# Re-ordering branch C of a two-layer decoder step: sample products into a gate, one linear between all pairs of levels

## The reference, cut to what matters

```
mix = gates_0 * (h_a @ w_pa) + gates_1 * (h_b @ w_pb) + gates_2 * (h_c @ w_pc)
x   = x + mix @ w_o
x   = x + (silu(gt) * up) @ w_down
```

## Time and profile before

| what | value |
| --- | --- |
| runs, us | 2079.83, 2083.93, 2085.56 (median 2083.93) |
| profiled execution, us | 2087.43 |
| its span, first to last instruction, us | 2085.4 |
| mean granted TensorE clock | 0.989 |
| instructions | 49973 |
| HBM traffic | 307.08 MB read, 12.08 MB written |

### The profile page before, as it was taken

The page is one execution under the profiler, slowest core; times in us unless marked ns, Lnnn a source line. Parts: engine busy times, 40 slices in busy tenths (PEclk is TensorE's granted clock), DMA queues, the critical chain, the costliest instruction groups (busy, mean ns, idle before and its releaser), DMA issues.

```text
span 2085.4 us, 49973 instructions
## 1 busy us (share of the span) xinstructions
PE 2038.4 (98%) x21064; PEld 1929.0 (92%) x21064; DVE 1043.7 (50%) x1611; ACT 720.2 (35%) x1135; POOL 298.0 (14%) x534
## 2 busy tenths in 40 slices
PE   8899999999999999999999999999999999999998
PEld 8888888889999999999998888888899999999998
DVE  7766523365756444433366654233666564444324
ACT  4444214156433222222234431142653332222221
POOL 0202456510000000000001034646000000000000
PEclk9999999999999999999999999999999999999999
DMA  6415999962333333333343279999414333333332
GB/s 220 125 56 167 305 345 335 344 205 72 128 102 91 93 91 92 92 89 89 98 161 103 83 232 301 354 315 356 128 56 136 103 91 89 99 91 92 86 93 77
DMA packets 165558, 322.44 MB, mean 155 GB/s; under 512 B 24420, under 2 KB 104855, under 8 KB 164823
## 3 DMA queue, kind: packets, MB, share of 16 engines
q10 hardware_dynamic: 46944, 147.87, 23.2%
q1 hardware_dynamic: 93814, 100.04, 14.6%
q0 software_dynamic: 24576, 71.34, 9.8%
HBM read 307.08 MB, written 12.08 MB: 153 GB/s over the span
## 4 chain that ended last, share of the span: by engine, by line
PE 85%; DVE 8%; ACT 3%; DMA 2%; issue 1%; ACTq 0%; SPq 0%; DVEq 0%
PE PS L1791 25%; PE PS L1793 24%; PE PS L1792 24%; PE PS L2034 3%; PE PS L2064 3%; DVE wl L686 1%; PE PS L2039 1%; PE PS L1844 1%; DMA vpg<-in_cache_vals 1%; ACT P L1461 1%; PE PS L1830 1%; DVE P L859 1%; DVE PTl L693 1%; DVE kxl L693 1%; DMA raw<-in_wpack 1%
## 5 line engine op out<-in xcount | busy, mean ns | idle before, releaser
L1791 PE MATMUL PS<-hh,wh 128*128 128x260 f32 x3008 | 865.4, 288 | 7.5 <-DVE wl L686 7.2
L1793 PE MATMUL PS<-hl,wh 128*128 128x260 f32 x3008 | 853.0, 284 | 0.0
L1792 PE MATMUL PS<-hh,wl 128*128 128x260 f32 x3008 | 852.2, 283 | 0.0
L1791 PEld LDWEIGHTS PS<-hh,wh 128*128 128x128 f32 x3008 | 570.1, 190 | 22.4 <-issue 13.2
L1793 PEld LDWEIGHTS PS<-hl,wh 128*128 128x128 f32 x3008 | 570.1, 190 | 0.0
L1792 PEld LDWEIGHTS PS<-hh,wl 128*128 128x128 f32 x3008 | 570.0, 189 | 0.1
L686 DVE TENSOR_TENSOR wl<-raw,wh 128x1024 fp32r<-128x1024 f32 (+4 forms) x326 | 359.4, 1103 | 315.3 <-ACT wh L1356 314.5
L1356 ACT ACTIVATE wh<-raw 128x1024 fp32r<-128x1024 f32 (+4 forms) x326 | 304.8, 938 | 464.2 <-PE PS L1793 454.0
L1791 PE MATMUL PS<-fh,wh 128*128 128x260 f32 x704 | 199.3, 283 | 0.0
L1793 PE MATMUL PS<-fl,wh 128*128 128x260 f32 x704 | 198.7, 282 | 0.0
L1792 PE MATMUL PS<-fh,wl 128*128 128x260 f32 x704 | 198.6, 282 | 0.0
(11 more groups left out here) (352 smaller groups left out, 3025.4 us busy)
## 6 DMA issues: line engine op xcount, KB each, us to landing
raw<-in_wpack ACTq DMA_DIRECT2D x238, 512.0 KB, 3.6
vpg<-in_cache_vals SPq DMA_DIRECT2D x256, 128.0 KB, 6.3
vpg<-in_cache_vals POOLq DMA_DIRECT2D x256, 128.0 KB, 5.4
kpg<-in_cache_keys SPq DMA_DIRECT2D x224, 144.0 KB, 4.3
kpg<-in_cache_keys POOLq DMA_DIRECT2D x112, 144.0 KB, 4.8
ky<-in_cache_keys POOLq DMA_DIRECT2D x96, 144.0 KB, 4.2
raw<-in_wpack ACTq DMA_DIRECT2D x48, 256.0 KB, 3.1
raw<-in_wpack ACTq DMA_DIRECT2D x16, 384.0 KB, 3.1
```

Of the source, the lines that this page charges most:

```text
L1791: pe.matmul(out, w[0], x[0], start=first, stop=False)
L1792: pe.matmul(out, w[1], x[0], start=False, stop=False)
L1793: return pe.matmul(out, w[0], x[1], start=False, stop=last)
```

## The change

It re-orders. No product, copy or transfer is added or taken away. In TensorE's queue oh and Ks0 move into g01, behind its fifth block of rows; then each pair of levels is followed by one linear: P00, g02, P01, g03, P02, g04, P03 (before: g01 L0 to L3 P00 and so on, with the sample products between levels). Kt is followed by g05, U by P04, oc0 by g06, the first sums by oc1 and P05, the second sums by g07. The list of groups is changed alike, so the banks move. VectorE's and ScalarE's queues are written anew to match; ScalarE's `sample_read(0)` comes ahead of the decays of its step, and its `head_guesses(0)` behind `outputs(1)` and `head_squares(1)`.

```diff
--- before.py
+++ after.py
@@ -291,21 +291,22 @@
 
     groups.extend(["Vt0", "Vt1", "D0", "D1", "Ot"])
     lin("g01")
-    between = (["oh", "Ks0"], ["P00", "Us0"], ["Ks1", "g02", "os0"], ["P01", "Us1"], ["g03", "os1"], ["P02"], ["g04"])
+    groups.extend(["oh", "Ks0"])
+    between = (["P00", "Us0"], ["Ks1", "g02", "os0"], ["P01", "Us1"], ["g03", "os1"], ["P02"], ["g04"], ["P03"])
     for n, names in enumerate(between):
         groups.extend([f"L{2 * n}", f"L{2 * n + 1}"])
         for name in names:
             (lin if name[0] in "gP" else groups.append)(name)
     groups.extend(["Kt0", "Kt1"])
-    lin("P03")
+    lin("g05")
     groups.extend(["U0", "U1"])
-    lin("g05")
+    lin("P04")
     groups.append("oc0")
-    lin("P04")
+    lin("g06")
     groups.extend(["no00", "no01", "oc1"])
-    lin("g06")
+    lin("P05")
     groups.extend(["no10", "no11"])
-    lin("P05", "g07", "P06", "P07", "g20", "g21")
+    lin("g07", "P06", "P07", "g20", "g21")
     for m in range(8):
         lin(f"P2{m}")
         if m < 6:
@@ -1141,39 +1142,30 @@
                 for k in range(2):
                     rows = brl[0][:, 2 * k:2 * k + 2, 0:TP]
                     lo(f"ha{k}", [(rows, rows.bitcast(F32), brh[0][:, 2 * k:2 * k + 2, 0:TP])])
+                sample_output()
+                spread_queries()
                 gate(0, 1)
                 for n in range(7):
                     if n < 5:
                         near(2 * n)
                         near(2 * n + 1)
-                    if n == 0:
-                        sample_output()
-                        spread_queries()
-                        weights(si["P00"])
-                    if n == 1:
-                        gated(0)
-                        sample_state(0)
+                    if n in (1, 3):
+                        merged(0, n // 2)
+                        sample_state(n // 2)
+                    elif n == 5:
+                        merged(0, 2)
+                    weights(si[("P00", "g02", "P01", "g03", "P02", "g04", "P03")[n]])
                     for i in (2 * n + 4, 2 * n + 5):
                         decayed(i)
                         if i + 3 < 16:
                             difference(i + 3)
-                    if n == 2:
-                        weights(si["g02"])
-                        gate(0, 2)
-                    elif n == 3:
-                        gated(1)
-                        sample_state(1)
-                    elif n == 4:
-                        weights(si["g03"])
-                        gate(0, 3)
-                    elif n == 5:
-                        gated(2)
-                    elif n == 6:
-                        weights(si["g04"])
-                        gate(0, 4)
+                    if n in (1, 3, 5):
+                        gate(0, 2 + n // 2)
+                merged(0, 3)
                 for p in range(2):
                     evac(f"Kt{p}", kbts[p][:, :, :].rearrange("p a b -> p (a b)"), bank(f"Kt{p}"))
-                gated(3)
+                weights(si["g05"])
+                gate(0, 5)
                 for p in range(2):
                     Sall = Salls[p]
                     dve.memset(Sall[:, 0, :], 0.0).then_inc(*mark("dve_step"))
@@ -1217,22 +1209,20 @@
                 def head_low(p, e, y):
                     lo(f"hc{p}{e}", [(brl[2][:, 2 * p + e, :], y[:, :], brh[2][:, 2 * p + e, :])])
 
-                weights(si["g05"])
-                gate(0, 5)
                 gated(4)
+                weights(si["g06"])
+                gate(0, 6)
                 head_variances(0)
+                weights(si["P05"])
                 head_roots(0)
                 ys = [head_output(0, e) for e in range(2)]
-                weights(si["g06"])
+                merged(0, 5)
                 for e in range(2):
                     head_low(0, e, ys[e])
-                gate(0, 6)
                 head_variances(1)
-                weights(si["P05"])
+                weights(si["g07"])
                 head_roots(1)
                 ys = [head_output(1, e) for e in range(2)]
-                merged(0, 5)
-                weights(si["g07"])
                 for e in range(2):
                     head_low(1, e, ys[e])
                 weights(si["P06"])
@@ -1657,50 +1647,53 @@
                 for p in range(2):
                     act.wait_ge(*upto(f"pe Vt{p}"))
                     act.activation(Vts[p][:, :, :, :].rearrange("p (a c) v w -> p a (c v w)", a=2), pair(f"Vt{p}", 512), ACT.Copy).then_inc(*mark("act_evac", f"free Vt{p}"))
+                weights(si["g01"])
+                for k in range(2):
+                    rows = brl[0][:, 2 * k:2 * k + 2, 0:TP].bitcast(F32)
+                    hi(f"ha{k}", [(brh[0][:, 2 * k:2 * k + 2, 0:TP], rows)], ["ha back"])
+                hi("ysm", [(brh[0][:, :, TP:T], ysm[:, :, :])], ["free oh"])
+                sample_keys(0)
+                gate(0, 1)
                 for n in range(7):
-                    weights(si[("g01", "P00", "g02", "P01", "g03", "P02", "g04")[n]])
+                    weights(si[("P00", "g02", "P01", "g03", "P02", "g04", "P03")[n]])
                     if n == 0:
-                        for k in range(2):
-                            rows = brl[0][:, 2 * k:2 * k + 2, 0:TP].bitcast(F32)
-                            hi(f"ha{k}", [(brh[0][:, 2 * k:2 * k + 2, 0:TP], rows)], ["ha back"])
-                        gate(0, 1)
-                        weights(si["P00"])
-                        hi("ysm", [(brh[0][:, :, TP:T], ysm[:, :, :])], ["free oh"])
-                        sample_keys(0)
                         decayed_state(0)
+                    elif n == 2:
+                        sample_read(0)
                     for i in (2 * n + 7, 2 * n + 8):
                         if i < 18:
                             decays(i)
-                    if n == 2:
+                    if n == 1:
                         sample_keys(1)
+                        gate(0, 2)
+                    elif n == 2:
                         decayed_state(1)
-                        gate(0, 2)
-                        sample_read(0)
+                    elif n == 3:
+                        gate(0, 3)
                     elif n == 4:
-                        gate(0, 3)
                         sample_read(1)
                     elif n == 5:
                         far(10)
                         far(11)
+                        gate(0, 4)
                     elif n == 6:
                         far(12)
                         far(13)
-                        gate(0, 4)
                 for p in range(2):
                     collected(p)
-                weights(si["P03"])
+                weights(si["g05"])
                 gate(0, 5)
+                weights(si["P04"])
                 outputs(0)
                 head_squares(0)
-                weights(si["P04"])
-                head_guesses(0)
+                weights(si["g06"])
+                gate(0, 6)
                 outputs(1)
                 head_squares(1)
-                weights(si["g06"])
+                head_guesses(0)
+                weights(si["P05"])
                 head_high(0)
-                weights(si["P05"])
                 head_guesses(1)
-                gate(0, 6)
                 weights(si["g07"])
                 head_high(1)
                 weights(si["P06"])
@@ -2256,35 +2249,38 @@
                 for k in range(2):
                     ins = turn(bank("Ot")[:, 128 * k:128 * k + 128], Oacc[:, 128 * k:128 * k + 128])
                 ins.then_inc(*mark("group_ready", "pe Ot"))
-                gate(0, 1)
+                def sample_part():
+                    sample_output()
+                    sample_keys(0)
+
+                gate(0, 1, {4: sample_part})
                 for n in range(7):
                     level(2 * n)
                     level(2 * n + 1)
                     if n == 0:
-                        sample_output()
-                        sample_keys(0)
-                    elif n == 1:
                         branch(0, 0)
                         sample_update(0)
-                    elif n == 2:
+                    elif n == 1:
                         sample_keys(1)
                         gate(0, 2, {4: lambda: sample_read(0)})
-                    elif n == 3:
+                    elif n == 2:
                         branch(0, 1)
                         sample_update(1)
+                    elif n == 3:
+                        gate(0, 3, {4: lambda: sample_read(1)})
                     elif n == 4:
-                        gate(0, 3, {4: lambda: sample_read(1)})
+                        branch(0, 2)
                     elif n == 5:
-                        branch(0, 2)
+                        gate(0, 4)
                     else:
-                        gate(0, 4)
+                        branch(0, 3)
                 for p in range(2):
                     begin(f"Kt{p}")
```

(9 more changed lines are left out.)

## The result

The changed kernel takes **2118.57 us** (median of 4 runs, 2116.19 to 2121.34), the kernel before beside it 2084.24 (4 runs, 2079.83 to 2085.56). The ratio is 1.0165, with an interval of 1.0146 to 1.0184: slower by 34 us, where 2117 were forecast. The profiled execution's span is 2119.7 us, 34.3 more than before, at a mean granted clock of 0.983 where it had been 0.989.

A forecast was written before the change was run, and what follows sets the result against it. TensorE, busy for 98% of the span, was taken to bound the kernel. Waits of +35.7 us, less 3.2 and 1.6, with clock -7 + 9.2, made +33, so a median of 2117 us; range 2102 to 2128.

The forecast's parts named there:

- the clock: TensorE's half-rate falls behind three pauses per layer: 4.6 us per layer, 9.2 in all, against 7 us of old ones removed.
- b): First level pairs: Ks1 waits for merged(0, 0), g02 for the addition of sample_state(0); 2.8 us lost per layer.
- c): After L6, L7: g03 takes P01's banks and waits for merged(0, 1) behind VectorE's copies; 1.4 us per layer.
- d): L10 takes os1's banks and waits for sample_read(1), put behind decays(15) and decays(16) on ScalarE; 1.6 us per layer.
- f): Heads, counted from T0, oc0's end: VectorE waits for ScalarE, making P06, P07 and g20 late; 11.9 us per layer.
- e): First sample read ahead of decays on ScalarE: Us1's copy comes in time, so 3.2 us of waits go.
- g): Costed at nothing: Kt, g05, U, P04, oc0, weight loads, the second half of S0 and POOL's clearing of blocks.
- The table load: On ScalarE: 1.28 us followed by its activation with no drain; with the skill's drain f would be 1.4 longer per layer.
- VectorE's work alone as what sets the heads: Rival 1: VectorE's own work makes g20 4.5 us late per layer, the sum 14.8 less; 2102 us, chance 0.08.
- The rival of 6.8 us falls: Rival 4: the falls of the clock are 6.8 us long behind each pause; 2128 us, chance 0.10.
- The faster rival: Rival 2: VectorE frees Ks1's and g02's banks and splits g20 in time, leaving 12 us of gains; 2072 us, chance 0.06.
- That gains and losses cancel: Rival 3: f vanishes, and a to d cost 12 us against 12 of gains; 2084 us, chance 0.04.

The follow-up runs named there:

- run with merge first: The changed kernel with merged and sample_state of the levels put ahead of the two near copies in VectorE's queue: 2104.21 us, ratio 1.0095.
- the run that takes this step alone: The kernel before with only sample_read(0) moved ahead of the state's scaling and the gate: 2080.55 us, ratio 0.9994.
- the exchange on ScalarE: The changed kernel with head_guesses(0) and the split of P06 ahead of outputs(1) and head_squares(1) in ScalarE's queue: 2105.21 us, ratio 1.0106.
- the run with the heads' queues mended: The changed kernel, TensorE's order kept, with splits of P06, P07, g20, g21, first guesses and P05's merge ahead of head work not needed yet: 2094.43 us.
- the one with only the heads: The kernel before with its old levels, but P03 ahead of Kt and the changed kernel's heads: 2110.51 us, ratio 1.013.
- the run with the old heads: The changed kernel's levels with the order of the kernel before from Kt on, in all queues: 2094.04 us, ratio 1.0053.
- the last run: The changed kernel's levels with merges and sample reads put forward, and the old order from Kt on: 2076.76 us, ratio 0.9968.
- The three runs with mended levels: The changed kernel with level merges and sample reads put forward; heads mended (2075.63 us), also P20 and g22 splits earlier (2073.41), or old heads (2076.76).

## Why the prediction was right, point by point

The direction and the places were right, and the total too; that the total is so close is in part luck, as the clock below shows. By its terms, per layer, forecast against measured in the first layer:

| term | forecast, us | measured, us |
| --- | --- | --- |
| a) L1 behind g01's gate read | 0.15 | 0.10 |
| b) Ks1, then g02 | 2.8 | 1.37 + 1.07 = 2.44 |
| c) g03 | 1.4 | 1.37 |
| d) L10 | 1.6 | 1.16 |
| f) P06, P07, g20 | 3.1, 2.3, 6.5 | 2.89, 2.02, 4.72 |
| sum of waits | 17.85 | 14.70 |
| clock, both layers, net | +2 | about +9 |

**b)** The order of VectorE's queue is as read: two copies, product, addition. The run with merge first shows it, for it removes the waits by an exchange in that queue alone. g02 starts 3.24 us behind L3's end (461.80 to 465.04), forecast 3.25. The two waits together are 0.4 smaller only because Ks1, at half rate, takes 0.80 us of it instead of 0.42.

**c)** holds to 0.03.

**d)** The releaser is right. The chain from g03's end to the copy took 5.51 instead of 5.8, beside 4.35 of TensorE instead of 4.2. Only the size was off, by 0.44.

**e)** In the changed kernel it is right: undoing it costs 11.7 us. But the sum books the -3.2 as a gain of its own, and the run that takes this step alone gains nothing that shows. A wait that is removed brings TensorE sooner to the next group, where 1.35 us of the 3.2 came back.

**f)** P06, P07 and g20 start 23.88, 29.01 and 38.36 us behind T0; the forecast had 23.8, 29.0 and 38.4. The chain through ScalarE's squares, table load and guesses into VectorE's queue is shown by the exchange on ScalarE, which cuts the idle time from 7.28 to 1.95 and leaves g20's wait. The three waits are 2.3 us less than forecast although the starts came as forecast, for two reasons: P07 ran at half rate and hides 1.5 of g20's, and TensorE's own work up to g20 is 27.2 instead of 26.5 (33.64 from T0 to P07's end, less 2.89, 2.02 and 1.5).

**g)** holds: the stretch has no wait that is not in the table.

**The table load.** The earlier trace rows do not show what the forecast reads from them: the activation behind that load, which they leave out, starts at 522.35, 1.64 us after the load's end, and waits for VectorE. The reading is right all the same. In ScalarE's timeline of the kernel before, at the load for the next sigmoid:

```profile
534.65 1.28 ACT L1524 ACT_TABLE_LOAD   x1
...
535.94 0.64 ACT L1524 ACTIVATE gsig<-gsig 128x520 f32<-128x520 f32 x1
```

and in that of the changed kernel, at the load of f:

```profile
537.70 1.28 ACT L1619 ACT_TABLE_LOAD   x1
539.00 0.64 ACT L1619 ACTIVATE rs<-var 128x520 f32<-128x520 f32 x1
```

The activation starts 0.01 and 0.02 us behind the load, and with f's starts right to 0.1 us there is no room for 1.4 more. The Trainium skill ("ScalarE: Activation LUTs", What ACT_TABLE_LOAD costs) gives about 1283 ns of load and about 1380 ns of drain for a switch: the load agrees with the 1.28 us here, the drain does not show in this case.

**The clock** is the term that was mis-sized. Per layer 23.9 us lie at half rate (6.8 behind Ks1, 6.8 behind g03, 3.4 in P07, 6.8 in g20), against 17.1 in both layers together before. Measured at like products: the first 30 matmuls of g02 take 5.50 us and those of g03 6.45, against 3.82 at full rate (g02 in the second layer of the kernel before), and g20 takes 7.97 against 6.02 (g06). That is 6.2 us, and with P07's 1.5 and Ks1's 0.4 it is 8.1 per layer where 4.6 were forecast. The forecast had three falls at 1.5 each; there are four, at 2.0. The waits were taken 6.3 us too large for two layers and the clock 7 us too small. More than half of that is one and the same time: the 1.5 at P07 and the 0.4 at Ks1 were forecast as waits and came as half rate, 3.8 us in two layers. That the rest, 2.5 against 3.2, cancels too is luck. With the measured terms, 2 x 14.70 of waits, -3.2 and -1.6, 2 x 8.1 of clock less the 7 of before make +33.8, against 34.3 of span.

**The rivals.** VectorE's work alone as what sets the heads (2102) is refuted, and more than by the number: its 4.5 us, which the range takes for the floor of f, were not a floor at all. The forecast kept the order of the queue when it counted VectorE's 22.6 us, though the second pair's roots and outputs are not needed until P20. Nor were the 22.6 all VectorE's own: from 540.71 to 563.15 here it takes 22.4, and 1.5 of them are its two gaps for ScalarE. The rival of 6.8 us falls (2128) was half true, three of four falls per layer are of that length, but the waits beside them were shorter. The faster rival (2072) named the two right places, Ks1 and g20: with both freed, and the late sample reads and P06 and P07 as well, the kernel takes 2075.63 and 2073.41. The argument against it, VectorE at 98% in rows 3, did not hold: the run with the heads' queues mended finds room in the heads. The gain was there in the new list of groups, in its levels, and the queues as written didn't deliver it. That gains and losses cancel (2084) is refuted by 34 us.

**Left open.** Whether P06's wait of "issue" is the one for the product of `merged(0, 5)`: the product ends 0.1 us ahead of P06's start in both the changed kernel and the one with only the heads, and it goes when that product comes earlier, but the profile names no releaser.

## What to carry to other kernels

A new order on the bound engine is half a change. For each group that is moved, look at what its slot waits for, and then at what stands ahead of that release in the other engines' queues; work that nothing needs yet must stand behind it. An engine that is busy for half of the span can still be late for every slot, and a floor by its total work says nothing until its queue has been put in the order of need. And a wait that is taken away alone is often worth less than its length, because the next release is late instead.

## What was not expected of the hardware

- The granted clock fell to 1.2 GHz for 6.8 us in pauses as short as 1.37 us (Ks1, g03) as well as in one of 4.72 (g20), and for 10.2 at one of 4.4. With the short ones removed it stayed at 2.4 GHz in three of the four places. At g03 the fall cost 2.6 us, twice the wait that it came with; in the run with the old heads the same wait of 1.37 came with a fall of only 3.4 us. In the changed kernel there was none at the wait of 2.89 of P06 or that of 1.16 of L10; in the run with merge first P06 ran at half rate behind the same wait of 2.89. So the length of a wait alone does not tell.
- A fall can hide a wait. P07 at half rate took 4.63 us where P06 took 3.11, and g20's wait was 4.72 where it is 6.22 to 6.25 in the kernels in which P07 is not slowed. Waits and clock can't be costed apart when the same release ends both.
- The clock falls without a wait, too, and not in the same places each time. In the run with merge first it fell in g03 of the second layer, in the last run in three windows in which TensorE was busy for 3.40 of 3.40 us. The three runs with mended levels have the same order of products there, and their profiled executions show none, one and three falls. These four and the one of the run with merge first all begin at g02 or g03, behind sample products and a level pair, from 1.2 us ahead of the linear's start to 0.3 after it. Two layers at 1.00 in one profile, against 0.97 and 0.96 before, do not show that the new order holds the clock.
